# Layer 1 attention: the query norm becomes the scale of the exponential, and the mask is written into the score banks by TensorE

## The reference

```python
def swa_mixer(qkv, q_norm, k_norm, sinks, cos, sin):
    q, k, v = split_cols(qkv, SWA_SIZES)
    q = apply_rope(rmsnorm(q.reshape(bsz, s, SWA_HEADS, SWA_HD), q_norm), cos, sin)
    k = apply_rope(rmsnorm(k.reshape(bsz, s, SWA_KV_HEADS, SWA_HD), k_norm), cos, sin)
    ...
    sc = jnp.einsum('bnqkgd,bnjkd->bnkgqj', qb, kb).astype(jnp.float32) * (SWA_HD ** -0.5)
    valid = (rel >= 0) & (rel < SWA_WINDOW) & (bidx * blk + kj - blk >= 0)
    sc = jnp.where(valid[None, :, None, None], sc, -jnp.inf)
    m = jnp.maximum(jnp.max(sc, axis=-1, keepdims=True), sink)
    p = jnp.exp(sc - m)
    denom = jnp.sum(p, axis=-1, keepdims=True) + jnp.exp(sink - m)
    o = jnp.einsum('bnkgqj,bnjkd->bqkgd', p / denom, vb.astype(jnp.float32))
```

## Time and profile before

| | us |
|---|---|
| median of 3 runs | 2776.22 |
| lowest, highest | 2773.38, 2781.71 |
| the profiled execution, its own time | 2772.21 |
| its span in the profile | 2770.0 |

### The profile page before, as it was taken

How to read it: one execution, slowest core, us unless ns; L and a number is a source line. 1 busy time by engine, 2 the same in 40 slices (tenths; PEclk the granted TensorE clock), 3 DMA queues, 4 the chain that set the end, 5 groups by cost and what they waited for, 6 DMA issues and landing times. The chain is left out here.

```text
span 2770.0 us, 46406 instructions
## 1 busy us (share of the span) xinstructions
PE 2643.6 (95%) x18376; PEld 2446.2 (88%) x18376; DVE 1788.6 (65%) x2468; ACT 1134.3 (41%) x1462; POOL 10.0 (0%) x18
## 2 busy tenths in 40 slices
PE   6898998999999999999999998889899999999999
PEld 5898898899898899889989997779788998899889
DVE  4666666655777755775576566765677646764774
ACT  2334434333444433443344434443344434443443
POOL 0000000000000000000000000000000000000000
PEclk8899999999999999999999999999899999999999
DMA  5343443355445665665556552225356655565564
GB/s 151 99 122 100 116 118 110 107 168 168 145 153 182 192 195 179 188 186 184 181 182 189 155 153 92 84 93 167 92 167 190 196 183 185 185 187 183 179 189 152
DMA packets 429633, 432.62 MB, mean 156 GB/s; under 512 B 15487, under 2 KB 427796, under 8 KB 429108
## 3 DMA queue, kind: packets, MB, share of 16 engines
q1 hardware_dynamic: 422832, 422.63, 49.5%
q0 software_dynamic: 1584, 5.40, 0.7%
q10 hardware_dynamic: 5076, 2.56, 0.3%
HBM read 428.44 MB, written 2.10 MB: 155 GB/s over the span
## 5 line engine op out<-in xcount | busy, mean ns | idle before, releaser
L875 DVE TENSOR_TENSOR w_lo<-w_raw,w_hi 128x1024 fp32r<-128x1024 f32 x800 | 965.8, 1222 | 582.9 <-ACT w_hi L476 579.3
L476 ACT CAST w_hi<-w_raw 128x1024 fp32r<-128x1024 f32 x800 | 834.4, 1047 | 830.7 <-PE stream L1458 488.7
L1471 PE MATMUL stream<-h,w_hi 128*128 128x512 f32 x2816 | 988.8, 397 | 0.0
L1472 PE MATMUL stream<-h,w_lo 128*128 128x256 f32 x2816 | 787.0, 279 | 0.0
L1471 PEld LDWEIGHTS stream<-h,w_hi 128*128 128x128 f32 x2816 | 528.8, 188 | 128.6
L1456 PE MATMUL stream<-act,w_hi 128*128 128x256 f32 x2016 | 581.0, 288 | 8.3 <-DVE act L902 8.3
L1458 PE MATMUL stream<-act,w_lo 128*128 128x256 f32 x2016 | 572.3, 284 | 0.0
L1457 PE MATMUL stream<-act,w_hi 128*128 128x256 f32 x2016 | 572.3, 284 | 0.0
L1472 PEld LDWEIGHTS stream<-h,w_lo 128*128 128x128 f32 x2816 | 530.8, 188 | 0.1
L1456 PE MATMUL stream<-h,w_hi 128*128 128x256 f32 x1536 | 464.7, 303 | 3.0 <-DVE w_lo L875 3.0
L1457 PE MATMUL stream<-h,w_hi 128*128 128x256 f32 x1536 | 439.9, 286 | 0.0
(11 more groups left out here) (339 smaller groups left out, 1767.0 us busy)
## 6 DMA issues: line engine op xcount, KB each, us to landing
w_raw<-in_ffn_in_w SPq DMA_DIRECT2D x352, 512.0 KB, 4.5
w_raw<-in_ffn_out_w SPq DMA_DIRECT2D x176, 512.0 KB, 4.4
w_raw<-in_hyb_in_w SPq DMA_DIRECT2D x96, 512.0 KB, 3.8
w_raw<-in_swa_in_w SPq DMA_DIRECT2D x48, 512.0 KB, 3.5
w_raw<-in_xkv_w SPq DMA_DIRECT2D x32, 512.0 KB, 3.4
w_raw<-in_hyb_out_w SPq DMA_DIRECT2D x32, 512.0 KB, 3.5
w_raw<-in_swa_out_w SPq DMA_DIRECT2D x32, 512.0 KB, 3.4
w_raw<-in_xq_w SPq DMA_DIRECT2D x16, 512.0 KB, 3.5
```

Of the source, the lines that this page charges most:

```text
L476: nc.scalar.copy(whi[:, k], raw[:, n % NRAW]).then_inc(hi_split, 1)
L875: v.tensor_tensor(wlo[:, k], raw[:, n % NRAW], whi[:, k].bitcast(F32), ALU.subtract).then_inc(lo_split, 1)
L1471: mm(bank[:, m, :], whi[:, k, kk, w], h[:, kt, :, :], start=(q == 0 and kk == 0), stop=False, skip_group_check=True)
L1472: last = mm(bank[:, m, 0:TOK], wlo[:, k, kk, w], h[:, kt, 0, :], start=False, stop=(q == 3 and kk == len(kts) - 1), skip_group_check=True)
```

## The change

It alters `swa_side` on ACT, DVE and PE, and adds five small DVE instructions in the stage before.

- The gain of the query norm and the factor 64^-0.5 go into a cosine table `q_cos` and a rotation matrix `q_rotm`, made once (tick 13 of the key and value stage). The rotation runs on the raw queries.
- The norm is no longer multiplied into the queries. It becomes a column per head and block: `rq`, 128 x 8, from four matmuls of 2 columns each in place of one of 512. It is the `scale` of the exponential.
- The mask goes into the score banks by 8 matmuls of the identity with the band (`ident_r`, `band_r`), and the scores are added on top. DVE takes the maxima straight from PSUM, the exponentials read PSUM too.
- Scores have other places in the banks (`score_cols`): even heads in B[2], odd heads in B[3], block 1 of heads 2 and 3 in B[4]. The matmuls alternate between partitions 0 to 63 and 64 to 127.
- Softmax is done in two halves, blocks 0 and 1, with a semaphore count each.
- The ticks move. Rotation 4g+4, scores and exponentials 4g+5, division of block 0 4g+7, of block 1 4g+8 (`swa_first`, ahead of the split), transposes 4g+8, copies 4g+9, values 4g+10, split of the result 4g+11. `SWA_LAST` is 41.

```diff
-SWA_LAST = 42
+SWA_LAST = 41
...
+            qcol = lp[:].rearrange("p a b -> p (a b)")
+            rq, neg_rq, rq_log, neg_sinks = qcol[:, 0:8], qcol[:, 8:16], qcol[:, 16:24], qcol[:, 32:32 + SWA_HEADS]
+            q_cos, q_rotm = ang[:, 0, :], ang[:, 1, 0:P]
+            band_r = wbah[:].rearrange("p k c -> p (k c)")
+            ident_r = wbal[:].rearrange("p k c -> p (k c)")[:, 0:P]
...
+        def score_cols(i, n):
+            if n == 0:
+                return B[2 + i % 2][:, i // 2 * P:i // 2 * P + P]
+            return B[2 + i][:, TOK:512] if i < 2 else B[4][:, (i - 2) * TOK:(i - 1) * TOK]
+        def score_pair(n):
+            both = BK[:, 2:4, n * TOK:n * TOK + TOK]
+            return both.rearrange("p b (k c) -> p b k c", k=2) if n == 0 else both
...
-                g = (t - 11) // 4
-                if t >= 11 and t == 4 * g + 11:
+                g = (t - 9) // 4
+                if t >= 9 and g < 8 and t == 4 * g + 9:
...
+                g = (t - 5) // 4
+                if t >= 5 and g < 8 and t == 4 * g + 5:
+                    for n in range(2):
+                        act.wait_ge(s_neg, 2 * g + n + 1)
+                        if g and n == 0:
+                            act.wait_ge(pt_done, g)
+                        for i in range(4):
+                            k = 4 * n + i
+                            src = score_cols(i, n)
+                            f(sc[:, i, 0:P] if n == 0 else sc[:, i, P:384], src, ACT.Exp, scale=rq[:, k:k + 1],
+                              bias=sst[:, 1, k:k + 1], accum_out=sst[:, 2, k:k + 1])
+                        f(sst[:, 4, 4 * n:4 * n + 4], sst[:, 3, 4 * n:4 * n + 4], ACT.Exp).then_inc(s_exp, 1)
...
-                    swa_rope(N_ROPE + 2 + g, 0, 4)
-                g = (t - 9) // 4
-                if t >= 9 and g < 8 and t == 4 * g + 9:
...
+                    ni = N_ROPE + 2 + g
+                    act.wait_ge(n_ss, ni + 1)
+                    act.wait_ge(n_out, ni)
+                    tables(LN_EXP)
+                    link(f(rq_log, B[0][:, 0:8], ACT.Ln, bias=eps_col, scale=1.0 / SWA_HD))
+                    f(rq, rq_log, ACT.Exp, scale=-0.5).then_inc(n_r, 1)
...
-                for lag in (7, 3, 5):
...
-                g = (t - 10) // 4
-                if t >= 10 and g < 8 and t == 4 * g + 10:
...
+            by_half = lambda ap: ap.rearrange("p (k b) -> p b k", b=2)
+            def shift(g, n):
+                h4 = slice(4 * n, 4 * n + 4)
+                link(v.tensor_tensor(sst[:, 0, h4], sst[:, 0, h4], neg_rq[:, h4], ALU.mult))
+                link(v.tensor_tensor(sst[:, 1, h4], sst[:, 0, h4], neg_sinks[:, 4 * g:4 * g + 4], ALU.min))
+                v.tensor_tensor(sst[:, 3, h4], sst[:, 1, h4], sinks[:, 4 * g:4 * g + 4], ALU.add).then_inc(s_neg, 1)
+            def softmax_in(g):
+                v.tensor_reduce(sst[:, 0, 4:6], score_pair(1), AX.X, ALU.max)
+                link(v.tensor_reduce(by_half(sst[:, 0, 0:4]), score_pair(0), AX.X, ALU.max))
+                shift(g, 0)
+                link(v.tensor_reduce(sst[:, 0, 6:8], two(B[4][:]), AX.X, ALU.max))
+                shift(g, 1)
+            def softmax_out(g, n):
+                h4 = slice(4 * n, 4 * n + 4)
+                k4 = slice(0, P) if n == 0 else slice(P, 384)
+                dve.wait_ge(s_exp, 2 * g + n + 1)
+                link(v.tensor_tensor(sst[:, 5, h4], sst[:, 2, h4], sst[:, 4, h4], ALU.add))
+                link(v.reciprocal(sst[:, 5, h4], sst[:, 5, h4]))
+                v.tensor_tensor(sc[:, :, k4], sc[:, :, k4], sst[:, 5, h4].unsqueeze(2).to_broadcast([P, 4, P + n * P]),
+                                ALU.mult).then_inc(s_prob, 1)
+            def swa_first(t):
                 g = (t - 8) // 4
                 if t >= 8 and g < 8 and t == 4 * g + 8:
+                    softmax_out(g, 1)
+            def swa_side(t):
+                g = (t - 7) // 4
+                if t >= 7 and g < 8 and t == 4 * g + 7:
+                    softmax_out(g, 0)
+                g = (t - 3) // 4
+                if g < 8 and t == 4 * g + 3:
+                    rope(3, N_ROPE + 2 + g, GROUP[SWQ] + g, SWQ + t, None, None, None)
+                g = (t - 4) // 4
+                if t >= 4 and g < 8 and t == 4 * g + 4:
+                    ni = N_ROPE + 2 + g
+                    dve.wait_ge(rot_done, g + 3)
+                    if g:
+                        dve.wait_ge(s_done, g)
+                    v.tensor_tensor(two(nr[:]), two(B[1][:]), sinb[:].unsqueeze(1).to_broadcast([P, 2, TOK]), ALU.mult)
+                    link(v.tensor_tensor(two(nraw[:]), two(nraw[:]), q_cos.unsqueeze(1).to_broadcast([P, 2, TOK]), ALU.mult))
+                    v.tensor_tensor(two(qf[:]), two(nraw[:]), two(nr[:]), ALU.add).then_inc(q_rot, 1)
+                    dve.wait_ge(n_r, ni + 1)
+                    link(refine(rq, rq_log, B[0][:, 0:8], SWA_HD))
+                    v.tensor_scalar(neg_rq, rq, -1.0, None, ALU.mult).then_inc(n_out, 1)
+                    dve.wait_ge(n_out, ni + 1)
+                g = (t - 5) // 4
+                if t >= 5 and g < 8 and t == 4 * g + 5:
                     dve.wait_ge(s_done, g + 1)
...
-                g = (t - 13) // 4
-                if t >= 13 and t == 4 * g + 13:
+                    softmax_in(g)
+                g = (t - 11) // 4
+                if t >= 11 and t == 4 * g + 11:
                     dve.wait_ge(pv_done, g + 1)
                     split_act(slice(2 * g, 2 * g + 2), two(B[5][:]), swa_out)
...
+                if t == 13:
+                    dve.wait_ge(trig_ready, 2)
+                    gain = pcol("swa_q_norm", 0)
+                    v.tensor_scalar(q_cos, cosb[:], gain, SWA_HD ** -0.5, ALU.mult, ALU.mult)
+                    v.tensor_scalar(q_rotm, c_("rot"), gain, SWA_HD ** -0.5, ALU.mult, ALU.mult)
+                    v.tensor_copy(ident_r, ident)
+                    v.tensor_copy(band_r, c_("band", 256))
+                    v.tensor_scalar(neg_sinks, sinks[:], -1.0, None, ALU.mult).then_inc(q_tables, 1)
+                    dve.wait_ge(q_tables, 1)
                 if t in (11, 15):
                     dve.wait_ge(kT_done, 2)
                     if t == 15:
                         dve.wait_ge(svT, 1)
                     evac_scaled(two(nraw[:]), 0, GROUP[SWKV] + g, SWKV + t)
             for t in range(32):
+                swa_first(t)
                 split(SWQ + t + AHEAD)
                 swa_side(t)
...
-                g = (t - 11) // 4
-                if t >= 11 and t == 4 * g + 11:
-                    pe.wait_ge(s_prob, g + 1)
+                g = (t - 4) // 4
+                if t >= 4 and g < 8 and t == 4 * g + 4:
+                    ni = N_ROPE + 2 + g
+                    pe.wait_ge(group_evac, GROUP[SWQ] + g + 1)
+                    if g:
+                        pe.wait_ge(q_rot, g)
+                    else:
+                        pe.wait_ge(q_tables, 1)
+                        pe.wait_ge(sv_ready, 2)
+                    mm(B[1][:], q_rotm, nraw[:], start=True, stop=True).then_inc(rot_done, 1)
+                    pe.wait_ge(n_sq, ni + 1)
+                    pe.wait_ge(n_out, ni)
+                    halves = c_("half")[:, 0:P:64]
+                    for n in range(TT):
+                        for m in range(2):
+                            o = 4 * n + 2 * m
+                            last = mm(B[0][:, o:o + 2], nsq[:, m * TOK + n * P:m * TOK + n * P + P], halves, start=True, stop=True)
+                    last.then_inc(n_ss, 1)
+                g = (t - 8) // 4
+                if t >= 8 and g < 8 and t == 4 * g + 8:
+                    pe.wait_ge(s_prob, 2 * g + 2)
                     for i in range(4):
                         for b in range(3):
                             k = 3 * i + b
                             last = transpose(B[2 + k // 4][:, (k % 4) * P:(k % 4) * P + P], sc[:, i, b * P:b * P + P])
                     last.then_inc(pt_done, 1)
-                g = (t - 7) // 4
-                if t >= 7 and g < 8 and t == 4 * g + 7:
-                    rope(7, N_ROPE + 2 + g)
-                g = (t - 12) // 4
-                if t >= 12 and t == 4 * g + 12:
+                g = (t - 5) // 4
+                if t >= 5 and g < 8 and t == 4 * g + 5:
+                    pe.wait_ge(q_rot, g + 1)
+                    if g:
+                        pe.wait_ge(pt_copied, g)
+                    else:
+                        pe.wait_ge(ksw_ready, 2)
+                    for i, n in ((0, 0), (2, 0), (0, 1), (1, 0), (3, 0), (1, 1), (2, 1), (3, 1)):
+                        mm(score_cols(i, n), ident_r, band_r if n else band_r[:, P:TOK],
+                           start=(i, n) in ((0, 0), (1, 0), (2, 1)), stop=False, skip_group_check=True)
+                    for i, n in ((2, 1), (1, 0), (0, 0), (3, 0), (2, 0), (1, 1), (0, 1), (3, 1)):
+                        half, q0 = i % 2, i // 2 * TOK + n * P
+                        rows = slice(64 * half, 64 * half + 64)
```

(24 more changed lines are left out.)

57 lines of the change are left out of this document (4 added, 53 removed).

## The result

The changed kernel takes 2747.9 us, the median of 4 runs (2747.2 to 2749.4), beside 2776.9 (2773.4 to 2781.7) for the kernel before on the same chip: a ratio of 0.990, 95% interval 0.9887 to 0.9913. The forecast was 2751 with a range of 2734 to 2765. The profiled execution took 2748.0 us, 24.2 less than that of before; its span is 2746.2 us.

A forecast was written before the change was run, and what follows sets the result against it. PE had most work but waited or ran at half clock. Periods gain 26.7, front 8.4, tail loses 6.1: 29.0, less 4 for half clock, 25 off the median 2776.2: 2751 us, range 2734 to 2765.

The forecast's parts named there:

- S and T: Points splitting each group's period: S is the end of the scores (first maximum), T the start of the transposes.
- part A: S to T, the softmax chain through DVE and ACT beside PE's work: forecast 13.7 us against 13.0 before.
- One sign of being wrong: In the stage: PE waiting for something other than DVE's division, such as the group from PSUM or `q_rot`.
- Front: Stage start, from the rotation at 1640.92 to the first S: 1649.1 instead of 1657.5, gain 8.4 us.
- tail: From the last S to the output projection's piece for the last `act` quarter: 27.8 us against 21.7, loss 6.1.
- Scores, the open price: Eight score matmuls per group in part B: between 1.3 and 3.1 us, taken as 2.4, midway.
- The row on the values: Profile row: value matmuls on two output-partition halves, 24 records in 1.73 us, where scores need 3.1 for 16.
- Mask and sums: PE per group: eight band matmuls 0.95 us in part B, four narrow head sums 0.9 us in part A.
- PE never waits: Rival: part A shorter than PE's work, period 20.1 us, total 2736, or 2728 with fast scores; chance 0.18.
- Half clock in each period: Rival at sums, wait and transposes: half clock costs 11 us, total 2758, 2764 with slow scores; chance 0.24 together.
- Slower: Rival: half clock through all of part B, doubling it to 15.5 us, period 29.2, total 2803; chance 0.04.
- part B: T to the next S, set by PE alone: forecast 7.75 us against 11.5 before.

The follow-up runs named there:

- fourth experiment: Changed kernel with ACT's and DVE's rounding and split of the second piece after the scores issued ahead of the exponentials and maxima: 2729.1 us, ratio 0.9808.
- second profile: The changed kernel run once more, unaltered, beside the changed kernel with one 512-column matmul for the sums of squares: 2744.2 us, ratio 0.9886.
- first experiment: Changed kernel with only the score order undone: four matmuls of the even heads first, then, after a wait, four of the odd heads: 2760.3 us, ratio 0.9931.
- fifth experiments: The kernel of the fourth experiment with the division of block 0 on DVE moved ahead of the split that waits for ACT: 2723.0 us, ratio 0.981.

## Why the prediction was right, and where it was not

**The split at S and T held.** The profile has S to T 14.02 us (forecast 13.7), T to S 6.96 (7.75), waits of 0.46 and 0.95 us in part A (0.3 and 1.1), and no wait of a piece for `act`. One sign of being wrong, as it was written down, did come: PE waits for the group from PSUM, 5.1 us in seven waits. The sum itself had 0.3 us of that wait in each period, so the sign was badly put, and the wait is 0.16 us longer than its term. That DVE stands idle until ACT has rounded came at 4.05 us (3.5), and that it is the price of moving the maxima ahead of two splits is shown by the fourth experiment: one split moved away makes T 1.14 us earlier.

**The sum.** Front 7.3 us (8.2), seven periods 150.5 (148.8), tail 1800.84 to 1829.06, 28.2 (27.8): 186.1 in all against 213.8, a gain of 27.8 where 25 was forecast. Without half clock the periods would have been 19.85 + 6 x 20.97 = 145.7 (19.85 is the first period of the changed kernel's second profile, at full clock). The forecast without it was 148.8, so 3 us better, and half clock took 4.8 us (3.2 in the first period, 1.6 in one other) where 4 us were set aside, part of them for the tail, which ran at full clock. The forecast time was missed by 3 us only (2747.9 and 2751). Part of that is luck: the scores came 6 us under their term, and a longer part A (0.3 us in each period) and more half clock took half of it back.

**Scores, the open price: mis-sized.** Taken at 2.4 us, midway, they measured 1.66, 0.74 us less in each of eight groups, 6 us in all. The term of sixteen loads at 0.1 us, 1.7, comes nearest. That the loads set the time is not shown. The row on the values was evidence that two halves work beside each other, and the midpoint gave it too little weight. The rule quoted from the Trainium skill, TensorEngine Tiling (Array Packing), Key Properties, agrees with the first experiment: the serial order takes 3.2 us, the alternating one 1.66. The 1.3 us that I drew from it were too low.

**Exponentials: two errors with opposite signs.** The forecast said that PSUM costs no more than SBUF and that a column as scale costs nothing. PSUM costs 0.05 us less, the column 0.09 more, each time. The net is some 0.04 x 8 = 0.3 us a period, which is the 0.3 by which part A was longer. I had seen the upper bound of 0.2 for the column and chosen zero, because the bias is a column already; the number as scale shows that this reason doesn't hold.

**Mask and sums: right.** The mask took 1.0 us by the timeline, 0.92 by its removal (0.95). The four 2-column sums (two records each) take 0.95 us, the wide one 1.02 by its row.

**The rivals.** "PE never waits", on the ground that ACT's split might come before the exponentials' end, did not happen by itself, but the fourth and fifth experiments brought it about: 19.13 us a period. I had put PE's own work at 20.1; with the scores at 1.66 that makes 19.4. "Half clock in each period" was half right: in the changed kernel 2 of 8 groups had it at 1.6 to 3.2 us, in the kernel with the values moved all seven periods. The prediction took the rule of the Trainium skill, TensorE: Matmul & The Clock Gate, Part 4, that transposes don't count as activity, as speaking for half clock in each period. Most transposes here ran at full clock behind 0.95 us of standstill, so the rule isn't enough to say when the clock falls. "Slower" did not come: it needed 7 us of half clock in part B of every period, and in the changed kernel one period had nearly that much (0.51 over 6 us, a part of it ahead of the transposes), one had half of it, and five had none.

**Where the gain comes from.** By the ratios, the values beside the softmax are worth 13 us (0.9947 - 0.990, of 2777), the alternating halves 9 (0.9931 - 0.990), each give or take some 6 us by the intervals. The two overlap, since both undone kernels also had more half clock. Less half clock is a part of the gain in the changed kernel too, by the windows up to 11 us. The mask on PE costs 0.92 us a group by its periods, 7 in all, and buys the shorter passes of DVE. What those are worth by themselves wasn't run.

## What to carry to other kernels

Where a chain through three engines runs beside a main engine, write down for both sides what stands between two points of the period. A change that leaves the chain as long as it was (13.0 us, then 14.0) still gains when more of the main engine's work lies beside it. Then look for an engine that stands idle right ahead of its part of the chain: here ACT had 5.7 us, and one piece of unrelated work put there brought a further 11 us in the periods, some 3 of them less half clock. With one division moved as well PE had no wait left, and a still shorter chain brought nothing.

## What the runs showed of the hardware

- fp32 matmuls whose inputs lie in the two halves of the partitions run beside each other if their order alternates: eight with 1536 columns in all take 1.66 us, and 3.2 us half after half with a wait between. The two halves wrote different banks at any one time; whether they have to was not run.
- An exponential with its sum takes, start to start, from PSUM 0.35 us (128 columns) and 0.45 (256) with a number as scale, 0.44 and 0.54 with a column; from SBUF 0.48 and 0.59 with a column.
- A wait of PE costs about 0.2 us more than the idle time in its row (19.13 us a period without waits, 19.83 with 0.53, 20.24 with 0.94).
- Four fp32 matmuls with 2 columns, eight records, take 0.95 us, about as long as one with 512 (1.02 by its row).
- The granted clock fell to 0.50 in some periods and not in others that look the same in every row, for 3 to 7 us at a time, in a place where PE had narrow matmuls, a wait and transposes. Behind waits of 0.94 or 0.95 us it did so in 11 of 36 periods, behind 0.88 with the wide sum in none of 12, and never in the steady periods of the three kernels whose waits there were 0.53 us or less. Behind the last wait of the stage, 2.0 to 4.6 us and without sums, it did in seven of nine profiles.
